# Grouping the 512- and 256-column products of a half panel, and four more panels in 512 columns

## What is computed

```
proj = rmsnorm(x) @ w_in          # 1024 -> 11 parts: fq, fk, fv, ff, gq, gk, gv, ga, gb, gz, gates
y_fox = softmax(fq fk^T * 128^-0.5 + decay, causal) fv        # 8 heads of 128
y_gdn = gated_delta_rule(silu(conv4(gq, gk, gv)), ...)        # 8 heads of 128
h = x + (sig(gate_f) * (y_fox @ Wf) + sig(gate_g) * (y_gdn @ Wg)) @ w_out
h = h + (silu(conv3(h' @ w_up)) ...) @ w_down
...second block: local attention, pooling, then
x = x + (silu(h2 @ w_gate) * (h2 @ w_up)) @ w_down
```

## Time and profile before

| | before |
|---|---|
| median of 3 runs | 804.54 us |
| the profiled execution's own time | 805.96 us |
| its span | 804.6 us |
| TensorE, matmuls busy | 797.8 us (99%), 5176 |
| TensorE, weight loads busy | 699.9 us (87%), 5176 |
| VectorE | 596.8 us (74%) |
| ScalarE | 448.1 us (56%) |
| GpSimd | 75.0 us (9%) |
| granted TensorE clock | 0.998 of full speed |

### The profile page before, as it was taken

One profiled execution on the slowest core, in us unless ns is written; L12 is line 12 of the kernel. 1 busy time (PEld: TensorE's weight loads), 2 busy tenths in 40 slices (PEclk: granted clock), 3 DMA queues, 4 the chain that ended last, 5 costly groups with the idle time before them and its releaser, 6 DMA issues.

```text
span 804.6 us, 13127 instructions
## 1 busy us (share of the span) xinstructions
PE 797.8 (99%) x5176; PEld 699.9 (87%) x5176; DVE 596.8 (74%) x1009; ACT 448.1 (56%) x727; POOL 75.0 (9%) x65
## 2 busy tenths in 40 slices
PE   8999999999999999999999999999999999999998
PEld 6888888999898888899999998887878888888886
DVE  6898989785555766679999996486766777778543
ACT  6577677554535544456656564366665655655431
POOL 0001000000011302101101110021100111011000
PEclk9999999999999999999999999999999999999999
DMA  9645564557442555475687665555425656656641
GB/s 316 185 158 158 166 231 147 161 145 227 122 119 89 171 173 203 162 241 177 199 247 243 216 202 196 175 186 175 142 82 170 203 176 205 196 172 208 194 151 74
DMA packets 118062, 144.09 MB, mean 179 GB/s; under 512 B 11489, under 2 KB 86641, under 8 KB 117745
## 3 DMA queue, kind: packets, MB, share of 16 engines
q1 hardware_dynamic: 115552, 141.22, 54.6%
q10 hardware_dynamic: 2448, 2.03, 1.1%
HBM read 141.78 MB, written 1.46 MB: 178 GB/s over the span
## 4 chain that ended last, share of the span: by engine, by line
PE 97%; DVE 1%; DMA 1%; ACT 0%; issue 0%; SPq 0%; DVEq 0%; ACTq 0%
PE bank L584 94%; PE bank L638 1%; DMA panel_raw<-in_w_in 1%; DVE conv_acc L1631 1%; PE bank L960 0%; PE bank L682 0%; PE bank L909 0%; DVE panel_lo L1595 0%; PE bank L933 0%; PE bank L660 0%; PE bank L737 0%; PE bank L839 0%; SPq L2400 0%; ACT panel_hi L1106 0%; DVE h L2024 0%
## 5 line engine op out<-in xcount | busy, mean ns | idle before, releaser
L1595 DVE TENSOR_TENSOR panel_lo<-panel_raw,panel_hi 128x1024 fp32r<-128x1024 f32 x245 | 308.0, 1259 | 138.9 <-ACT panel_hi L1106 138.5
L584 PE MATMUL bank<-x_halves,panel_hi 128*128 128x256 f32 (+1 forms) x1536 | 368.3, 322 | 0.7 <-DVE x_halves L2031 0.7
L1106 ACT ACTIVATE panel_hi<-panel_raw 128x1024 fp32r<-128x1024 f32 (+1 forms) x247 | 260.4, 1055 | 176.6 <-PE bank L584 174.6
L584 PE MATMUL bank<-x_halves,panel_lo 128*128 128x256 f32 x1024 | 289.1, 282 | 0.0
L584 PEld LDWEIGHTS bank<-x_halves,panel_hi 128*128 128x128 f32 x1536 | 257.0, 191 | 23.3 <-issue 0.9
L584 PEld LDWEIGHTS bank<-x_halves,panel_lo 128*128 128x128 f32 x1024 | 195.7, 191 | 0.2
L584 PE MATMUL bank<-panel_hi,x_halves 128*128 128x512 f32 x384 | 122.0, 399 | 0.0
L584 PEld LDWEIGHTS bank<-panel_hi,x_halves 128*128 128x128 f32 x384 | 70.0, 188 | 14.4 <-DVE panel_lo L1595 0.6
L584 PE MATMUL bank<-panel_lo,x_halves 128*128 128x512 f32 x192 | 75.1, 391 | 0.0
L584 PE MATMUL bank<-panel_hi,act_hi 128*128 128x512 f32 x176 | 68.6, 390 | 0.0
L584 PE MATMUL bank<-panel_hi,act_lo 128*128 128x512 f32 x176 | 68.5, 389 | 0.0
(11 more groups left out here) (291 smaller groups left out, 913.1 us busy)
## 6 DMA issues: line engine op xcount, KB each, us to landing
panel_raw<-in_w_in SPq DMA_DIRECT2D x35, 1024.0 KB, 5.3
panel_raw<-in_w_up SPq DMA_DIRECT2D x30, 1024.0 KB, 5.2
panel_raw<-in_w_down SPq DMA_DIRECT2D x20, 1024.0 KB, 5.0
panel_raw<-in_w_gate SPq DMA_DIRECT2D x10, 1024.0 KB, 5.3
panel_raw<-in_w_out SPq DMA_DIRECT2D x8, 1024.0 KB, 5.1
panel_raw<-in_w_in SPq DMA_DIRECT2D x11, 512.0 KB, 5.5
panel_raw<-in_w_branch_fox SPq DMA_DIRECT2D x4, 1024.0 KB, 5.0
panel_raw<-in_w_branch_gdn SPq DMA_DIRECT2D x4, 1024.0 KB, 5.1
```

What stands on the lines that cost most here:

```text
L584: return e.matmul(o, l, r, start=start, stop=stop, skip_group_check=True)
L1106: return e.activation(o, i_, ACT.Copy, scale=scale)
L1595: e.tensor_tensor(lo, raw_view(i, k0, kt), hi.bitcast(F32), ALU.subtract).then_inc(s_lo, 1)
```

## The change

It does three things. The last four panels fq2, fk2, fq3, fk3 go from fm to hl; with them come a ring of banks 4, 1, 0, a buffer for the copied right half, a copy by ScalarE (`fqk_low_copy`) in place of `fox_project`, a scaled sum by VectorE (`fqk_sum`), and the side ring without bank 4 during these steps. In every hl step, the old 64 and the new 8, TensorE now makes the eight products of 512 columns first and then the eight of 256. And in such a step it waits for `panel_hi` ahead of the first eight and for `panel_lo` only ahead of the second.

```diff
-            add((kind, j), "mix", True, "w_in", 0, KD, c0 + j * PW)
+            out.append(((kind, j), "mix", "hl" if j >= 2 else "fm", "w_in", 0, KD, c0 + j * PW, PW))
...
+FQK = [(kind, j) for j in (2, 3) for kind in ("fq", "fk")]
...
+        fqk_low = [at(f"fqk_low{i}", [P, 2, T], 17.5, skip=2048 * i) for i in range(2)]
...
-        rings = {"few": [0, 1], "conv": [4, 0, 1], "fox": [2, 3], "side": [4, 5, 6, 7], "gemm": [0, 1, 2, 3]}
+        rings = {"few": [0, 1], "fqk": [4, 1, 0], "conv": [4, 0, 1], "fox": [2, 3], "side": [4, 5, 6, 7], "gemm": [0, 1, 2, 3]}
...
                     if j == 0:
-                        e.wait_ge(*landed)
+                        e.wait_ge(*((s_hi, n) if how == "hl" else landed))
...
                         if how == "hl":
                             mm(o, hi[:, k, js], HALVES_OF[x][:, :, kx, :], begin and k == 0, False)
-                            i_ = mm(o[:, 0:T], lo[:, k, js], xh[:, kx, :], False, last and k == kt - 1)
                             continue
...
+                if how == "hl":
+                    e.wait_ge(s_lo, n)
+                    for j in range(2):
+                        for k in range(kt):
+                            i_ = mm(bank_of(targets[j])[:, 0:T], lo[:, k, j * P:(j + 1) * P], xh[:, kp + k0 + k, :], False,
+                                    last and k == kt - 1)
+                        if last and j == 0:
+                            i_.then_inc(will_fill(targets[0]), 1)
                 i_.then_inc(s_half, 1)
...
-                e.wait_ge(*emptied(("fq", hh // 2)))
-                e.wait_ge(*emptied(("fk", hh // 2)))
+                for kind in ("fq", "fk"):
+                    e.wait_ge(*emptied((kind, hh // 2, hh % 2) if (kind, hh // 2) in FQK else (kind, hh // 2)))
...
+                if n == FIRST_HALF["fq", 2] + 1:
+                    rings["side"] = [5, 6, 7]
+                if n == END["fk", 3] + 2:
+                    rings["side"] = [4, 5, 6, 7]
...
+            def fqk_low_copy(kind, j):
+                p = FQK.index((kind, j))
+                for m in range(2):
+                    if p >= 2:
+                        e.wait_ge(*emptied((*FQK[p - 2], m)))
+                    e.wait_ge(*product_of((kind, j), m))
+                    copy(fqk_low[p % 2][:, m, :], bank_of((kind, j, m))[:, T:2 * T],
+                         float(DH) ** -0.5 if kind == "fq" else 1.0).then_inc(s_fqk_low, 1)
...
+            def fqk_sum(kind, j, m):
+                p = FQK.index((kind, j))
+                dst, scale = (qfT, float(DH) ** -0.5) if kind == "fq" else (kfT, 1.0)
+                e.wait_ge(s_fqk_low, 2 * p + m + 1)
+                e.scalar_tensor_tensor(dst[:, 2 * j + m, :], bank_of((kind, j, m))[:, 0:T], scale,
+                                       fqk_low[p % 2][:, m, :], ALU.mult, ALU.add).then_inc(empties((kind, j, m)), 1)
```

More of the change, by code:

```diff
@@ L450, in build @@
         s_yf_hi = sem("yf_hi")
+        s_fqk_low = sem("fqk_low_copied")
         s_gate_f, s_gate_g, s_mixed, s_y_hi = (sem(n) for n in ("gate_f_affine", "gate_g_affine", "mixed", "y_hi"))
@@ L511, in ring_of @@
                 return "fox"
+            if key in FQK:
+                return "fqk"
             if key in CONVS and CONVS.index(key) in CONV_BOTH:
@@ L625, in gemm @@
                             i_ = mm(o, l, r, begin and k == 0 and m == 0, last and k == kt - 1 and m == 2)
-                    if two and last and j == 0:
+                    if how == "wide" and last and j == 0:
                         i_.then_inc(will_fill(targets[0]), 1)
+                if how == "hl":
[6 more added lines that the diff above has]
+                            i_.then_inc(will_fill(targets[0]), 1)
                 i_.then_inc(s_half, 1)
@@ L1414, in scalar_program @@
                         if n == END[kind, j]:
-                            fox_project(kind, j)
+                            (fqk_low_copy if (kind, j) in FQK else fox_project)(kind, j)
                 for c in range(2):
@@ L2046, in vector_program @@
                 split(n + 3)
+                for kind, j in FQK:
+                    if n == END[kind, j]:
+                        fqk_sum(kind, j, 0)
                 if n == 13:
@@ L2189, in vector_program @@
                                                ALU.subtract).then_inc(empties(("yg", b)), 1)
+                for kind, j in FQK:
+                    if n == END[kind, j]:
+                        fqk_sum(kind, j, 1)
                 if n - 5 in FOX_AT:
```

## The result

| | before | changed |
|---|---|---|
| median | 804.49 us, 13 runs | 805.94 us (805.73 to 807.42), 13 runs |
| ratio | | 1.0017, 95% interval 1.0010 to 1.0024 |
| span of the profiled execution | 804.6 us | 804.6 us |
| TensorE, products | 5176 | 5112 |
| VectorE | 596.8 us | 600.2 us |

The changed kernel is 1.45 us slower, 0.18%. The interval lies just above a ratio of 1, so the direction is clear, though the size is under the 0.2% that the prediction took as the least that can be told. The forecast was 805.3 us, range 803.0 to 807.3, "within 0.2%" at 0.73.

What follows compares the result with a forecast made beforehand. TensorE was taken as the bound, its time being product count times spacing. Terms -0.70 + 0.88 - 0.54 + 1.36 - 0.2 = +0.8 us, put on the 804.54 us median, gave 805.3 us; range 803.0 to 807.3.

Steps and rivals of the forecast that it cites:

- The grouped half: One hl step on TensorE, eight products of 512 columns then eight of 256: 2.793 us, between 2.773 and 2.825.
- (b): Second block's 44 hl steps: grouping adds a restart to steps already at the plain sum, +0.88 us.
- (a): Four panels moved from fm to hl, 8 steps: 24 products become 16 at equal columns, -0.70 us.
- (c): First block's 20 hl steps: grouping replaces the mostly slow alternating pace of 2.825 us, -0.54 us.
- (d): First block's q and v panels: second bank needed sooner, so TensorE waits in steps 11, 17 and 31, +1.36 us.
- (e): Start of an hl step at 98 us: waiting for panel_hi alone removes the one panel_lo wait, -0.2 us.
- (f): Steps 49 to 56: added VectorE sums (3.4 us) and ScalarE copies fit beside TensorE, cost 0.
- Settled runs: Two rivals, restart perhaps not paid every step: 803.9 us with bank waits (chance 0.12), 802.5 without (0.07).
- The dear restart: Rival: every grouped half takes 2.825 us, decided in the second block; 807.6 us, chance 0.19.
- Loads that do not hide: Rival: each TensorE weight load takes its own 0.135 us, so 64 fewer give 8.7 us back; 795.9 us, chance 0.01.
- The new wait in steps 49 to 56: Rival: fk2's second bank comes late and TensorE waits, about +0.5 us; 805.8 us, chance 0.03.
- The sign that was named for the waits: Timeline check: product 5 behind a gap in steps 11, 17, 31; conv_tmp releases TensorE at about 1.5 us, not 0.6.

## Why the prediction was right

**The grouped half** was priced at 2.793 us. Forty take 741.87 - 630.13 = 111.74, so 2.7935. The seams of the earlier trace rows were the right rows, and half the restarts cost half as much (2.783). Four short runs in a step cost 0.013 and not the 0.032 that the same seams would give, so the price holds for runs of eight.

**(b)** predicted +0.88 for 44 steps; +0.81 in the 40 steps 191 to 230, and nearly nothing (+0.02) in the four ahead. Steps 188 to 190 got 0.02 longer each, but step 187 got 0.04 shorter: the old order ran it at the slow pace, and the new one pays no restart there, since a run of 512 columns stands ahead of it.

**(a)** predicted -0.70, measured -0.61 (and -0.55 alternating). These steps stand behind small work, so their first gap is longer, 0.31 to 0.42 us where an fm step had 0.20 to 0.30. But that gap grew by 0.90 us over the eight steps, just as the settled figures give (0.91). What is missing lies behind it: the further gaps of the old fm steps add up to 21.07 us and not the 21.12 of settled ones, those of the new steps to 19.55 and not 19.52.

**(c) and (d)** together were +0.82 and are +1.29: right in kind, too small. Steps 11 and 17 came out at +0.47 and +0.48 against 0.48 each. Step 31 took +0.56 against 0.40, and step 23, where I had written that at v0 and v2 "the new due time is still level with the sum or behind it", took +0.20. At step 23 the prediction's own estimate was nearly right (it set the bank level with the product), but it left out what a wait costs once it happens: the first product behind one is followed after 0.335 to 0.338 us and not after 0.227. Steps 11 and 17 had paid that before the change. Step 23 pays it anew, and step 31 about half of it, since its ninth product had been followed after 0.286 us even before. The rest beyond the prediction is lateness of about 0.1 in each. The pace of the other steps gave 1.71 - 1.29 = 0.42 back, against 0.54.

**(e)** failed: no gain. The wait for `panel_lo` at 98 us was not what held the step. The load's idle time there is 0.2 us in both traces; only the name changed, and the run with the wait put back shows no difference.

**(f)** held: TensorE waits nowhere in steps 49 to 56, and 3.4 us more of VectorE cost nothing that shows.

**The rivals.** Settled runs (803.9, 802.5) are out: each restart is paid anew. The dear restart (807.6) is out for grouped steps, though its price, 2.825, is real for alternating ones. Loads that do not hide (795.9) are out. The 0.135 us used there is the busy time of all loads, overlaps counted once, over their number; one load lasts 0.19 us on the page, and products still follow each other in 0.120. The new wait in steps 49 to 56 (805.8) came nearest in number, but there is no such wait in the trace.

The sum +0.8 should have been +1.4: 0.47 from (c) and (d), 0.2 from (e), 0.09 from (a), less 0.07 in (b) and 0.08 in steps that the sum did not touch. The signs of the large terms and their places were right. That the measured +1.45 lay inside the range owes something to its width: it reached from 1.5 us under the kernel before to 2.8 above. The sign that was named for the waits was too small as well: loads waited 3.0 us for `conv_tmp`, in four steps, where 1.5 in three had been written.

## What to carry to other kernels

Where TensorE is the bound and its products follow each other without a gap, order decides a few nanoseconds a product: measure the pace of a run from first and last starts, and ask what stands at its seams before regrouping it. Regrouping also moves the moment at which each bank is first touched; where that bank is freed by another engine's late work, half a microsecond saved ahead of a wait is half a microsecond lost behind it. A change that loses in sum may hold a part that gains: here the four panels in 512 columns, and grouping only where the old pace was slow.

## What the runs showed of the hardware

- An alternating run of 512 and 256 columns showed two steady paces, 0.347 and 0.353 us a pair, at full clock and with no wait, and kept the one that it had for as long as nothing interrupted it (39 steps at the slow one here). Behind an unbroken run of equal products it took the slow one (steps 5, 9, 15, 21, 27 and 187 of before, 192 above); behind small products of other work it took either (in before steps 10, 188 and 190 fast, eight others slow). In step 31 of before the slow pace changed to the fast one at one late product, 0.286 us behind the one ahead. What sets the pace inside TensorE stays open.
- A run of eight products of 512 columns behind 256 columns took 0.027 us more than a settled one in each of the steps 191 to 230; with four runs of two in a step, the step took 0.013 more.
- The first product behind a wait for a bank was followed 0.11 us later than usual, in all four such steps of the changed kernel and in steps 11 and 17 of before. It was the same behind an idle 0.49 us (step 11) and behind a start only 0.13 us late (step 23), so a short wait costs nearly as much again as it lasts.
